# Value phase of a two-layer decoder trunk: a fifth slot for streamed expert weights, three buffers for the activations' high half, and a smaller dynamic DMA scratch

## The reference, cut to what matters

```python
def peer_ffn(h, w_q, sub_keys, u, v):
    ...
        eidx = jnp.take_along_axis(cidx, pos, axis=-1)
        g = jax.nn.softmax(sc, axis=-1)
        act = jax.nn.gelu(jnp.einsum('bchkd,bcd->bchk', u[eidx], hb).astype(jnp.float32))
        return jnp.einsum('bchk,bchkd->bcd', (g * act).astype(hb.dtype), v[eidx])
```

## Time and profile before

| | us |
|---|---|
| median of 3 runs | 2414.97 |
| lowest, highest | 2414.66, 2416.52 |
| span of the profiled execution | 2416.1 |
| value phase of layer 0, first to last start of a matmul | 864.5 to 1211.3 |
| value phase of layer 1, first to last start of a matmul | 2068.0 to 2412.4 |

### The profile page before, as it was taken

The page is one execution under the profiler, slowest core; times in us unless marked ns, Lnnn a source line. Parts: engine busy times, 40 slices in busy tenths (PEclk is TensorE's granted clock), DMA queues, the critical chain, the costliest instruction groups (busy, mean ns, idle before and its releaser), DMA issues.

```text
span 2416.1 us, 43695 instructions
## 1 busy us (share of the span) xinstructions
PE 2387.7 (99%) x17453; PEld 2215.8 (92%) x17453; DVE 1914.6 (79%) x3222; ACT 1442.9 (60%) x2123; POOL 790.2 (33%) x452
## 2 busy tenths in 40 slices
PE   9999999999999999999999999999999999999999
PEld 8999999999999988888898999999999999888887
DVE  7988787499489975899778887875984899768996
ACT  5586664444677754656555966644446777556663
POOL 0011410288888820000000113003888888100000
PEclk9999999999999999999999999999999999999999
DMA  7633345355544455666555332454555444566654
GB/s 257 220 123 123 119 143 187 138 184 184 175 161 162 158 192 193 211 202 225 186 192 194 132 129 107 150 189 139 184 181 176 160 158 159 192 200 208 200 192 157
DMA packets 104169, 419.26 MB, mean 174 GB/s; under 512 B 11680, under 2 KB 12192, under 8 KB 87072
## 3 DMA queue, kind: packets, MB, share of 16 engines
q1 hardware_dynamic: 103968, 416.47, 50.8%
HBM read 415.38 MB, written 1.05 MB: 172 GB/s over the span
## 4 chain that ended last, share of the span: by engine, by line
PE 84%; DVE 6%; ACT 4%; DMA 3%; issue 2%; POOL 1%; SPq 0%; DVEq 0%; ACTq 0%
PE banks L407 18%; PE banks L2279 18%; PE banks L409 18%; PE banks L408 18%; PE banks L2261 3%; DMA xr<-in_xstream 2%; PE banks L2295 2%; PE banks L2296 2%; PE banks L2294 2%; DVE ring_lo L382 1%; DVE xr_lo L1876 1%; ACT xr_hi L1871 1%; PE banks L867 1%; DMA ring<-in_wstream 1%; POOL xr_lo L1876 1%
## 5 line engine op out<-in xcount | busy, mean ns | idle before, releaser
L1876 POOL TENSOR_TENSOR xr_lo<-xr,xr_hi 128x1024 fp32r<-128x1024 f32 x256 | 620.1, 2426 | 389.3 <-ACT xr_hi L1871 388.8
L1871 ACT ACTIVATE xr_hi<-xr 128x1024 fp32r<-128x1024 f32 x460 | 485.3, 1056 | 377.0 <-DMA xr<-in_xstream 376.5
L407 PE MATMUL banks<-featH,xr_hi 128*128 128x256 f32 x2048 | 576.4, 281 | 1.8 <-POOL xr_lo L1876 1.8
L408 PE MATMUL banks<-featL,xr_hi 128*128 128x256 f32 x2048 | 575.4, 281 | 0.0
L409 PE MATMUL banks<-featH,xr_lo 128*128 128x256 f32 x2048 | 575.2, 281 | 0.0
L407 PEld LDWEIGHTS banks<-featH,xr_hi 128*128 128x128 f32 x2048 | 385.7, 188 | 2.8 <-POOL xr_lo L1876 1.9
L409 PEld LDWEIGHTS banks<-featH,xr_lo 128*128 128x128 f32 x2048 | 386.1, 189 | 0.0
L408 PEld LDWEIGHTS banks<-featL,xr_hi 128*128 128x128 f32 x2048 | 386.1, 189 | 0.0
L407 PE MATMUL banks<-featH,ring_hi 128*128 128x256 f32 x1232 | 351.7, 285 | 2.0 <-DVE ring_lo L382 1.8
L408 PE MATMUL banks<-featL,ring_hi 128*128 128x256 f32 x1232 | 346.9, 282 | 0.0
L409 PE MATMUL banks<-featH,ring_lo 128*128 128x256 f32 x1232 | 346.5, 281 | 0.0
(11 more groups left out here) (416 smaller groups left out, 4725.2 us busy)
## 6 DMA issues: line engine op xcount, KB each, us to landing
xr<-in_xstream SPq DMA_DIRECT2D x460, 512.0 KB, 3.3
ring<-in_wstream SPq DMA_DIRECT2D x128, 1024.0 KB, 4.9
b_raw<-in_xstream SPq DMA_DIRECT2D x104, 256.0 KB, 3.6
smw<-in_small SPq DMA_DIRECT2D x4, 617.0 KB, 10.0
first<-in_wstream SPq DMA_DIRECT2D x4, 512.0 KB, 5.7
first<-in_wstream SPq DMA_DIRECT2D x2, 1024.0 KB, 9.3
subk<-in_subkeys SPq DMA_DIRECT2D x2, 1024.0 KB, 7.0
x<-in_x SPq DMA_DIRECT2D x2, 512.0 KB, 5.6
```

The source lines that it names most:

```text
L407: PE.matmul(o, s_hi_lo[0], m_hi_lo[0], start=first, stop=False)
L408: PE.matmul(o, s_hi_lo[0], m_hi_lo[1], start=False, stop=False)
L1871: A.activation(xr_hi[:, m % XR], xr[:, m % XR], ACT.Copy).then_inc(s_xhi, 1)
L1876: (PO if m < NKEY else V).tensor_tensor(xr_lo[:, m % XR], xr[:, m % XR], xr_hi[:, m % XR].bitcast(F32), ALU.subtract).then_inc(s_xlo_pool ...
```

## The change

It adds a fifth slot for value units. Value unit n uses slot n % 5; the first five still come after key units in the slots 0 to 3. The fifth slot is a separate piece of memory behind `acts` (`extra_at`), with 4 KB a partition for the high half and 4 KB shared by weight and low half. From value unit 5 on, a load waits for the unit five before it (`slot_free`), and value unit 4 waits for nothing of its own. The position of the seven's pieces in SP's list is kept relative to `done`, so it comes one unit load later in the list. `x_hi` and `x_lo` stay three units ahead in the programs of ACT and DVE.

The activations' high half gets a third buffer (2 KB a partition, behind the fifth slot). Pairs 0 to 2 are made before the phase, and at even i pair i // 2 + 2. The wait of a pair is the same in number of units at the same i: `VU + 2 * (r - 3) + 2` with r one larger.

The dynamic DMA scratch goes from its default to 1024 bytes.

```diff
+XV = 5
+def slot_of(m):
+
+    return m % XR if m < NKEY else (m - NKEY) % XV
+def slot_free(m):
+
+    if m < NKEY + XR:
+        return m - XR + 1
+    return m - XV + 1 if m >= NKEY + XV else 0
...
+            extra_at = layer_at + EXPERT_SMALL + 4 * NKEY * S
+            xv_hi = alias("xv_hi", [P, D], F32R, offset=extra_at)
+            xv = alias("xv", [P, D], F32, offset=extra_at + 4 * D)
+            xv_lo = alias("xv_lo", [P, D], F32R, offset=extra_at + 4 * D)
...
                 if m >= XR:
-                    sp.wait_ge(s_xu, past(s_xu) + m - XR + 1)
+                    sp.wait_ge(s_xu, past(s_xu) + slot_free(m))
...
-                p_hi = alias("p_hi", [P, 2, 2, S], F32R, offset=hot_at)
+                p_hi = [alias(f"p_hi_{i}", [P, 2, S], F32R, offset=at)[:] for i, at in
+                        enumerate((hot_at, hot_at + 8 * S, extra_at + 8 * D))]
...
-                    return r % 2
+                    return p_hi[r % 3]
...
-                        done = m - XR + 1 - VU
+                        done = m - XV + 1 - VU
...
-                            if r >= 2:
-                                act.wait_ge(s_xu, past(s_xu) + VU + 2 * (r - 2) + 2)
+                            if r >= 3:
+                                act.wait_ge(s_xu, past(s_xu) + VU + 2 * (r - 3) + 2)
...
-                    for r in range(2):
+                    for r in range(3):
                         p_hi_pair(r)
...
-                            p_hi_pair(i // 2 + 1)
+                            p_hi_pair(i // 2 + 2)
...
-                    for r in range(2):
+                    for r in range(3):
                         p_lo_pair(r)
...
-                            p_lo_pair(i // 2 + 1)
+                            p_lo_pair(i // 2 + 2)
...
-    nc = bacc.Bacc("TRN2", target_bir_lowering=False, num_devices=1)
+    nc = bacc.Bacc("TRN2", target_bir_lowering=False, num_devices=1, dynamic_dma_scratch_size=1024)
```

More of the change, by code:

```diff
@@ L117, with slot_loads @@
 SEVEN_AT = tuple(2 * r - 2 * j for j, r in enumerate(SEVEN))
-def slot_loads(i):
-    return sum(m % XR == i for m in range(NKEY + ONE_BY_ONE))
+def slot_of(m):
+    return m % XR if m < NKEY else (m - NKEY) % XV
+def slot_loads(i, until=NKEY + ONE_BY_ONE):
+    return sum(slot_of(m) == i for m in range(until))
+def slot_free(m):
+    if m < NKEY + XR:
+        return m - XR + 1
+    return m - XV + 1 if m >= NKEY + XV else 0
 PER_LAYER = {
@@ L135 @@
     "expert_weights_loaded_2": 16 * slot_loads(2), "expert_weights_loaded_3": 16 * slot_loads(3),
+    "expert_weights_loaded_4": 16 * slot_loads(4),
     "seven_loaded_0": 64 * SEVEN_SET.count(0), "seven_loaded_1": 64 * SEVEN_SET.count(1), "seven_hi": 4 * len(SEVEN),
@@ L290, in trunk @@
         s_chosen, s_gt, s_gttk = sem("experts_chosen"), sem("choice_turned"), sem("choiceT_taken")
-        s_xl = [sem(f"expert_weights_loaded_{i}") for i in range(XR)]
+        s_xl = [sem(f"expert_weights_loaded_{i}") for i in range(XV)]
         s_xhi, s_xlo_pool, s_xlo_dve = sem("expert_weight_hi"), sem("expert_weight_lo_pool"), sem("expert_weight_lo_dve")
@@ L1853, in layer_programs, with x_parts @@
             assert (PIECES - 4) % RING == 2 and 2 * XR * D == RING * WCOL
+            extra_at = layer_at + EXPERT_SMALL + 4 * NKEY * S
+            xv_hi = alias("xv_hi", [P, D], F32R, offset=extra_at)
+            xv = alias("xv", [P, D], F32, offset=extra_at + 4 * D)
+            xv_lo = alias("xv_lo", [P, D], F32R, offset=extra_at + 4 * D)
+            def x_parts(m):
+                i = slot_of(m)
+                return (xr[:, i], xr_hi[:, i], xr_lo[:, i]) if i < XR else (xv[:], xv_hi[:], xv_lo[:])
             def x_load(sp, m):
                 if m >= XR:
-                    sp.wait_ge(s_xu, past(s_xu) + m - XR + 1)
+                    sp.wait_ge(s_xu, past(s_xu) + slot_free(m))
                 else:
@@ L1861, in x_load @@
                 unit = m if m < NKEY else NKEY + PLAIN[m - NKEY]
-                sp.dma_start(xr[:, m % XR], xstream[layer * (2 * NKEY) + unit]).then_inc(s_xl[m % XR], 16)
+                sp.dma_start(x_parts(m)[0], xstream[layer * (2 * NKEY) + unit]).then_inc(s_xl[slot_of(m)], 16)
             def x_hi(act, m):
@@ L1867, in x_hi @@
                     return
-                act.wait_ge(s_xl[m % XR], past(s_xl[m % XR]) + 16 * (m // XR + 1))
+                act.wait_ge(s_xl[slot_of(m)], past(s_xl[slot_of(m)]) + 16 * slot_loads(slot_of(m), m + 1))
                 if m >= XR:
-                    act.wait_ge(s_xu, past(s_xu) + m - XR + 1)
-                A.activation(xr_hi[:, m % XR], xr[:, m % XR], ACT.Copy).then_inc(s_xhi, 1)
+                    act.wait_ge(s_xu, past(s_xu) + slot_free(m))
+                w, hi, _ = x_parts(m)
+                A.activation(hi, w, ACT.Copy).then_inc(s_xhi, 1)
             def x_lo(eng, m):
                 eng.wait_ge(s_xhi, past(s_xhi) + m + 1)
-                (PO if m < NKEY else V).tensor_tensor(
-                    xr_lo[:, m % XR], xr[:, m % XR], xr_hi[:, m % XR].bitcast(F32), ALU.subtract
-                ).then_inc(s_xlo_pool if m < NKEY else s_xlo_dve, 1)
+                w, hi, lo = x_parts(m)
+                (PO if m < NKEY else V).tensor_tensor(lo, w, hi.bitcast(F32), ALU.subtract
+                                                      ).then_inc(s_xlo_pool if m < NKEY else s_xlo_dve, 1)
             ffn = ExitStack()
@@ L2274, in value @@
                         m, unit = VU + i, PLAIN[i]
-                        ph = p_hi[:, pslot(i // 2), i % 2, t * P:(t + 1) * P]
+                        ph = pslot(i // 2)[:, i % 2, t * P:(t + 1) * P]
+                        _, high, low_part = x_parts(m)
                         pl = acts_lo[unit // QUARTER][:, unit % QUARTER, t * P:(t + 1) * P]
-                        for p, w, first_one, last in ((ph, xr_hi, True, False), (ph, xr_lo, False, False), (pl, xr_hi, False, True)):
+                        for p, w, first_one, last in ((ph, high, True, False), (ph, low_part, False, False), (pl, high, False, True)):
                             for h in halves:
-                                mm = PE.matmul(bank[2 * t + h][:], p, w[:, m % XR, h * 512:(h + 1) * 512],
+                                mm = PE.matmul(bank[2 * t + h][:], p, w[:, h * 512:(h + 1) * 512],
                                                start=first_one and i == 0, stop=last and i == ONE_BY_ONE - 1)
@@ L2371, in p_hi_pair @@
                             unit = PLAIN[2 * r]
-                            if r >= 2:
-                                act.wait_ge(s_xu, past(s_xu) + VU + 2 * (r - 2) + 2)
+                            if r >= 3:
+                                act.wait_ge(s_xu, past(s_xu) + VU + 2 * (r - 3) + 2)
                             if unit == EARLY:
                                 act.wait_ge(s_gated, past(s_gated) + LATE_PAIRS)
-                            A.activation(p_hi[:, pslot(r)], acts[:, unit:unit + 2, :], ACT.Copy).then_inc(s_phi, 1)
+                            A.activation(pslot(r), acts[:, unit:unit + 2, :], ACT.Copy).then_inc(s_phi, 1)
                     def b_high(j):
@@ L2570, in p_lo_pair @@
                             V.tensor_tensor(acts_lo[unit // QUARTER][:, i:i + 2, :], acts[:, unit:unit + 2, :],
-                                            p_hi[:, pslot(r)].bitcast(F32), ALU.subtract).then_inc(s_plo, 1)
+                                            pslot(r).bitcast(F32), ALU.subtract).then_inc(s_plo, 1)
                     def first_sums(j):
```

## The result

| | before | changed |
|---|---|---|
| median, us | 2414.97 (5 runs) | 2403.07 (5 runs) |
| lowest, highest | 2414.20, 2416.52 | 2401.82, 2403.88 |
| span of the profiled execution | 2416.1 | 2401.1 |
| value phase of layer 0, first to last matmul start | 346.8 | 340.1 |
| value phase of layer 1 | 344.4 | 340.1 |

The ratio on record is 0.9946, 95% interval 0.9936 to 0.9957, which is 10.4 to 15.5 us; the two medians differ by 11.9 us.

A forecast was written before the change was run, and what follows sets the result against it. PE, busy 99% of the span, was taken as the bound, so only its stops could be gained. Of 10.4 us lost, minus 1, plus 0.3, minus 0.5 gave 9.2: 2414.97 to 2405.8 us, range 2403.8 to 2410.6.

The forecast's parts named there:

- 0 for the third pair at the start: Start of a value phase: the third activation pair's extra ACT and DVE work fits existing slack and costs 0.
- 0 for the scratch: Smaller dynamic DMA scratch: costs 0, since all data passes over the hardware queue and POOL issues no transfer.
- 0.3 us at the end of layer 0: Layer 0's tail: the split of the next layer's first weights ends earlier, so DVE's add starts 0.3 us sooner.
- Sum: Total: 10.4 less about 1 for unevenness, plus 0.3 at the layer's end, less 0.5 for small delays: 9.2 us gained.
- the 10.4: Both value phases: PE's total loss in us against an even pace of 0.2275 per matmul, 6.4 plus 4.0.
- upper bound of 10.7: Whole kernel: the most the change was expected to gain, in us; the lower bound was 6.8.
- Third buffer: Activations' high half in value phases: deadline moves by 5.46 us, ending nine stops on the low half even without the fifth slot.
- Fifth slot: Value unit loads go out one unit, 2.73 us, earlier; ACT waits less and DVE's split comes earlier by as much.
- the 3.3 us: Median unit load from issue to landing, against which the 5.12 us load before PE's longest stop was held.
- The first (the stops pass on to the weights and half stays): Value phases: bandwidth holds loads around the seven's pieces, stops pass to weights, half the gain stays: 2410.4 us; chance 0.13.
- The second (DVE takes it back): Value phases: DVE becomes the bound and takes all the gain back: 2415 us; chance 0.05.
- The third (scratch): SP's transfers: 1024 bytes of scratch leave only one in flight, slowing value units to about 2531 us; chance 0.03.

The follow-up runs named there:

- the run with the pieces spread: Kernel before, with two of the next seven's four weight pieces issued after the next unit load instead of four in a row: 2413.99 us, ratio 0.9986.

## Why the prediction was right and wrong

**Right: what bounds it, and that every stop in the phases would go.** PE's waits on both low halves are gone in both phases, the rest is as it was, and the start of a phase stayed covered. Taking 0 for the third pair at the start was right: it cost DVE 0.6, which the slack covered. In the changed kernel the first low half lasted 2.40 us, from 856.77 to 859.16, while POOL's last subtraction ran to 858.62, and the other two lasted 0.68 each. A rule of the Trainium skill (SBUF — State Buffer, Who interferes with whom) said that DVE with two SBUF inputs is blocked until GpSimd's instruction ends: by that rule nothing more would be lost once POOL was done, and the trace agrees. 0 for the scratch was right too (ratio 0.9999, interval 0.9990 to 1.0007).

**Right: 0.3 us at the end of layer 0.** The split of the next layer's weights no longer holds the add. From the last value matmul to the next layer's first product it takes 2.65 us in all three profiles with early loads and a tail of three, and 2.92 to 2.97 in the six with loads as before: 0.3.

**Wrong: the size, in the step "Sum".** Three parts of it:

1. I took 1 us of the 10.4 off "as unevenness that no buffer touches" and 0.5 "for small delays that stay". Both were there to be had. After the change no distance between two matmuls of a phase is over 0.24 us; before, 24 and 21 were, and these 45 held 10.0 of the 10.9 us lost, though only 11 of them count as stops of PE. A good part of the others comes from the same late low halves: PEld, the weight load, waited for the activations' low half 22 times (6.6 us in 11 waits in layer 0, 4.7 in 11 in layer 1), where PE's rows name 9, and these waits are gone after the change. The last 0.9 us were spread over shorter delays, and went too.
2. The pace. 62.80 / 276 = 0.2275 is the mean of a stretch that is richer in sevens than a whole phase. The same 276 matmuls take 62.81 us in both traces, so rounding isn't the cause; matmuls of plain units follow each other at 0.2267 and those of most sevens at 0.2312. The undisturbed phase has 340.1 / 1496 = 0.2273, which adds 0.3 us a layer: in the first pair of profiles the phases lost 691.2 - 680.3 = 10.9, not 10.4.
3. One profile. The stops depend on when single loads land, and that differs by execution. The four profiles with the old timing of loads have sums of 691.2, 692.2, 692.3 and 693.2, mean 692.2. The first was the lowest of them. Against 680.3 the loss is **12.0 us**, with 0.3 at the layer's end 12.3; measured were 11.9, 13.4 and, for five slots alone, 13.1, each with an interval several us wide. My upper bound of 10.7 was no bound, since it came from one execution's sum.

**Wrong: which part does it.** In the step "Third buffer" I wrote that without the fifth slot this would end the nine stops that name the activations' low half. By name it does, but PE then waits for the weights: 7.2 us of 12 are gained. The step "Fifth slot" was right in its mechanism and undersold: I counted it as what keeps stops from passing on, and it does all of it alone.

**Read wrongly: the 3.3 us.** In the paragraph on why it stops I held the load of 5.12 us against a median of 3.3, which is that of the whole program. In the phase itself the median was 3.9 and the longest load 6.1, so 5.12 was less exceptional than I wrote. That a load waits longer beside the seven's pieces was argued from one row; the run with the pieces spread shows it for the median load and not for the longest ones.

**The rivals.** The first (the stops pass on to the weights and half stays) is what three buffers alone do, not the change; its premise, that loads are held by bandwidth and not by their slot, is wrong in the main: 2.73 us of earlier issue cost 0.4 us of longer loads at the median. The second (DVE takes it back) didn't occur: 58.28 of 62.80 busy as before. The third (scratch) is excluded by its own run.

## What to carry to other kernels

When a stop names one operand, look at what stands before that operand's producer in its engine's order: here the activations were late because the engines ahead of them stood waiting for weights, and starting the loads one unit earlier removed every stop with no change to the activations. A gain from removing stops that hang on landing times should be summed from more than one profile; one gave 10.9 us here, four gave 12.0. Subtract nothing for "unevenness" unless a stretch without stops shows it too. And take the price of a load from the stretch at hand: 3.3 us in the whole program was 3.9 in this phase.

## What the runs showed that I had not expected

A single unit load can take 5.63 us where the median of its phase is 3.4, with nothing but other unit loads issued in the 15 us before it. The granted clock fell to its lower level for 3.4 us in the middle of one execution, after an idle of 1.79 us of PE; in the nine other profiles it didn't fall at that place, where PE's longest idle was 0.86 us. An idle of that length doesn't always bring it down: in the run with the pieces spread PE stood idle 1.83 us before 2125.47, and the granted clock stayed at the upper level.
